# Stage ends, first products and the final scaling of a two-layer streaming encoder reordered, and the inverse row sums spread by ScalarE

## What is computed

```python
def sink_softmax(logits, sink):
    m = jnp.maximum(jnp.max(logits, axis=-1, keepdims=True), sink)
    p = jnp.exp(logits - m)
    return p / (jnp.sum(p, axis=-1, keepdims=True) + jnp.exp(sink - m))

def conv_ffn(x, left, g, w_gate, w_up, cw, cb, w_down):
    xn = rms_norm(x, g)
    a = xn @ w_gate
    ap = jnp.concatenate([left, a], axis=1)
    ac = cb + sum(ap[:, j:j + L] * cw[j] for j in range(CONV_W))
    return (jax.nn.gelu(ac) * (xn @ w_up)) @ w_down, ap[:, -(CONV_W - 1):]

# per layer: h = h + attention(rms_norm(h)) @ w_o ; h = h + conv_ffn(h)
# end: rms_norm(h, g_final)
```

## Time and profile before

| | us |
|---|---|
| median of 3 runs (2988.56 to 2990.41) | 2989.19 |
| profiled execution | 2989.44 |
| its span | 2987.7 |
| TensorE busy | 2881.6 |
| prompts, layers 0 and 1 | 208 and 319 |

### The profile page before, as it was taken

How to read it: one execution, slowest core, us unless ns; L and a number is a source line. 1 busy time by engine, 2 the same in 40 slices (tenths; PEclk the granted TensorE clock), 3 DMA queues, 4 the chain that set the end, 5 groups by cost and what they waited for, 6 DMA issues and landing times. The chain is left out here.

```text
span 2987.7 us, 47694 instructions
## 1 busy us (share of the span) xinstructions
PE 2881.6 (96%) x18405; PEld 2707.4 (91%) x18405; DVE 1521.5 (51%) x2719; ACT 676.0 (23%) x1324; POOL 902.0 (30%) x861
## 2 busy tenths in 40 slices
PE   7999999999999999999888999999999999999997
PEld 6987798999999999988588777789999999999996
DVE  5046615544444444445588777532644444444445
ACT  3035511000000000013466655532100000000002
POOL 4233333222222222224123754323222222222221
PEclk8999999999999999999999999999999999999998
DMA  4430011111111111114012000021111111111111
GB/s 122 65 96 10 21 29 36 37 37 40 42 42 42 42 42 42 42 35 129 1 35 72 10 11 9 20 79 36 36 43 42 42 36 41 42 42 42 35 35 73
DMA packets 178196, 129.66 MB, mean 43 GB/s; under 512 B 25313, under 2 KB 168353, under 8 KB 177846
## 3 DMA queue, kind: packets, MB, share of 16 engines
q1 hardware_dynamic: 178066, 127.90, 14.9%
HBM read 111.13 MB, written 15.16 MB: 42 GB/s over the span
## 5 line engine op out<-in xcount | busy, mean ns | idle before, releaser
L665 DVE TENSOR_TENSOR h<-h,ps_gemm 128x1170 f32<-128x1170 f32 x192 | 263.7, 1373 | 407.8 <-PE ps_gemm L1433 232.4
L1195 POOL CAST w_hi<-w_raw 128x1024 fp32r<-128x1024 f32 x120 | 125.1, 1042 | 1130.2 <-PE ps_gemm L1417 624.9
L1417 PE MATMUL ps_gemm<-xh,w_hi 128*128 128x390 f32 x1920 | 448.1, 341 | 0.0
L1417 PE MATMUL ps_gemm<-xh,w_lo 128*128 128x390 f32 x1920 | 448.1, 342 | 0.0
L1417 PE MATMUL ps_gemm<-xl,w_hi 128*128 128x390 f32 x1920 | 446.1, 340 | 0.0
L1417 PEld LDWEIGHTS ps_gemm<-xh,w_hi 128*128 128x128 f32 x1920 | 352.5, 189 | 0.0
L1417 PEld LDWEIGHTS ps_gemm<-xl,w_hi 128*128 128x128 f32 x1920 | 349.4, 189 | 0.0
L1417 PEld LDWEIGHTS ps_gemm<-xh,w_lo 128*128 128x128 f32 x1920 | 349.1, 189 | 0.0
L1198 POOL TENSOR_TENSOR w_lo<-w_raw,w_hi 128x1024 fp32r<-128x1024 f32 x120 | 288.1, 2401 | 17.4
L1381 PE MATMUL ps_gemm<-xl,w_hi 128*128 128x390 f32 (+1 forms) x1152 | 272.5, 345 | 0.0
L1433 PE MATMUL ps_gemm<-gu_lo,w_hi 128*128 128x390 f32 x1056 | 248.7, 344 | 0.0
(11 more groups left out here) (393 smaller groups left out, 4346.5 us busy)
## 6 DMA issues: line engine op xcount, KB each, us to landing
w_raw<-in_w_gate SPq DMA_DIRECT2D x44, 512.0 KB, 3.8
w_raw<-in_w_up SPq DMA_DIRECT2D x44, 512.0 KB, 3.8
w_raw<-in_w_down SPq DMA_DIRECT2D x44, 512.0 KB, 3.3
w_raw<-in_w_in_b SPq DMA_DIRECT2D x13, 512.0 KB, 4.1
w_raw<-in_w_qkv_a SPq DMA_DIRECT2D x10, 512.0 KB, 4.0
residual_park<-h SPq DMA_DIRECT2D x1, 4680.0 KB, 13.7
h<-residual_park SPq DMA_DIRECT2D x8, 585.0 KB, 8.2
out<-yt SPq DMA_DIRECT2D x9, 512.0 KB
```

Source lines behind the costliest of these rows:

```text
L665: dve.tensor_tensor(c3(h[:, m, :]), c3(h[:, m, :]), pse(j), ALU.add).then_inc(evac[j % 2], 1)
L1195: pool.tensor_copy(whi[c % 3][:], raw[c % 2][:]).then_inc(w_hi_done, 1)
L1417: mm = pe.matmul(ps[j % 2][:, m_, 0:CH], w[:, k, :], x[:, k, m_ * CH:(m_ + 1) * CH], start=(k == 0 and w is wh and x is XH), stop=(k == KT ...
```

## The change

- `gemm` with `gate`: for all eight channel tiles first the two products with XH (waiting for `xh_done`), then the product with XL (waiting for `xl_done`). In the norms ahead of the feed-forward networks the addition of the seventh square moves behind the third low half.
- Feed-forward: the GELU is multiplied by R before the up product is there; the product is then taken out of PSUM times that, in three pieces. The last loop iteration is written out; context transposes stand in it in three groups of two, taken by VectorE alone. `last_down` starts its first two output blocks with the first hidden tile of the pair before it waits for the second.
- Attention: ScalarE copies the inverse row sums to a 128x128 block (`repeat_inverse`), TensorE transposes that in place of the two matmuls; VectorE's reciprocal waits for an older copy.
- Index stage: `take_qi(2)` and `take_qi(3)` stand three score additions earlier.
- End: transposes and VectorE's multiplication by the gain start before the mean of squares is known; all first halves go first, ScalarE scales them later; second halves as before. The last square is not added but summed by a second matmul.

```diff
+            dve.memset(gb[:, T - 2:T], 0.0).then_inc(pad_ga, 1)
             def up(F, u, j, i):
-                wait_at(dve, gul_done, F, 2, i)
-                wait_at(dve, mm_done, j + 1, 12, i)
-                dve.tensor_tensor(c3(gb[:]), pse(j), c3(R[:]), ALU.mult).then_inc(evac[j % 2], 1)
-                wait_at(dve, evac[j % 2], j // 2 + 1, 6, i)
-                wait_at(dve, gel_done, F + 1, 2, i)
-                dve.tensor_tensor(gb[:, 0:MAIN], gb[:, 0:MAIN], ac[:, 0:MAIN], ALU.mult)
-                dve.tensor_tensor(gv, gv, acs, ALU.mult).then_inc(prod_done, 1)
+                wait_at(dve, gel_done, F + 1, 2, i)
+                dve.tensor_tensor(ac[:, 0:MAIN], ac[:, 0:MAIN], R[:, 0:MAIN], ALU.mult)
+                dve.tensor_tensor(acs, acs, Rs, ALU.mult).then_inc(ac_scaled, 1)
+                wait_at(dve, gul_done, F, 2, i)
+                wait_at(dve, ac_scaled, F + 1, 2, i)
+                wait_at(dve, mm_done, j + 1, 12, i)
+                dve.tensor_tensor(gb[:, 0:2 * CH]..., src[:, 0:2, 0:CH], ac[:, 0:2 * CH]..., ALU.mult)
+                dve.tensor_tensor(gb[:, 2 * CH:MAIN], src[:, 2, 0:MAIN - 2 * CH], ac[:, 2 * CH:MAIN], ALU.mult)
+                dve.tensor_tensor(gv, src[:, 2, ...], acs, ALU.mult).then_inc(evac[j % 2], 1)
...
             def pair(F, jb, i, ctx):
...
                 for m in range(3, KT):
                     residual(dve, jb + 1 + m, m, i)
+                ctx(0)
                 up(F, 0, jb + 9, i)
+                ctx(2)
                 gate(F + 1, 1, jb + 10, i)
                 up(F + 1, 1, jb + 11, i)
+                ctx(4)
...
             def gemm(c, j, x_hi, x_lo, n=P, gate=None, between=None):
+                if gate is not None:
+                    for k in range(KT):
+                        pe.wait_ge(xh_done, gate + k + 1)
+                        for w in (wh, wl):
+                            for m in range(NCH):
+                                pe.matmul(..., w[:, k, 0:n], x_hi[:, k, ...], ...)
+                    for k in range(KT):
+                        pe.wait_ge(xl_done, gate + k + 1)
+                        for m in range(NCH):
+                            mm = pe.matmul(..., wh[:, k, 0:n], x_lo[:, k, ...], ...)
...
-                ctx_transposes(m // 2, g_ctx)
-                down(c0 + 4 + 6 * it, jb + 12 * it, 0, gu0 + FT)
+                job(c, jl, 0, 0)
+                down(c + 1, jl + 1, 0, gu0 + FT - 2)
+                ctx_transposes(m // 2, g_ctx, 0)
+                job(c + 3, jl + 9, 0, 0)
+                ctx_transposes(m // 2, g_ctx, 2)
+                job(c + 4, jl + 10, 0, 0)
+                job(c + 5, jl + 11, 0, 0)
+                ctx_transposes(m // 2, g_ctx, 4)
+                last_down(c + 6, jl + 12, gu0 + FT)
+            def last_down(c, j, f_done):
...
+                pe.wait_ge(gul_done, f_done - 1)
+                for m_ in range(2):
+                    pe.wait_ge(evac[(j + m_) % 2], (j + m_) // 2)
+                    products(m_, 0)
+                pe.wait_ge(w_split, c + 2)
+                pe.wait_ge(gul_done, f_done)
+                for m_ in range(KT):
+                    if m_ >= 2:
+                        pe.wait_ge(evac[(j + m_) % 2], (j + m_) // 2)
+                        products(m_, 0)
+                    products(m_, 1).then_inc(mm_done, 1)
...
-                            pe.wait_ge(p_rinv, NU * layer + i + 1)
-                            for r in range(2):
-                                mm = pe.matmul(tb[j % 2][HD * r:HD * (r + 1), P * k:P * (k + 1)],
-                                               stat(2, i, r).to_broadcast([P, HD]), ident[:], start=True, stop=True)
+                            pe.wait_ge(p_wide, NU * layer + i + 1)
+                            mm = pe.transpose(tb[j % 2][:, P * k:P * (k + 1)],
+                                              inverse(layer, i).rearrange("p r d -> p (r d)"), ident[:])
...
+                def repeat_inverse(i):
+                    act.wait_ge(p_rinv, NU * layer + i + 1)
+                    if i >= 2:
+                        act.wait_ge(p_tr, transposed(layer, i - 2))
+                    copy(inverse(layer, i), stat(2, i).unsqueeze(2).to_broadcast([P, 2, HD])).then_inc(p_wide, 1)
...
                     part(parts[1])
+                    if 1 <= n <= NU:
+                        repeat_inverse(n - 1)
                     if n < NU:
                         probs(n, 1)
...
                         dve.wait_ge(p_exp, 2 * (NU * layer + n))
+                        if n >= 4:
+                            dve.wait_ge(p_wide, NU * layer + n - 3)
                         dve.reciprocal(stat(2, n - 1), stat(1, n - 1)).then_inc(p_rinv, 1)
...
-                for n in range(half // 2 * i, half // 2 * (i + 1)):
+                n0, n1 = half // 2 * i, half // 2 * (i + 1)
+                for n in range(n0, n1 - 3):
                     add_scores(n)
                 take_qi(2 + i)
+                for n in range(n1 - 3, n1):
+                    add_scores(n)
...
+            for gi in range(3):
+                turn_final(gi)
+            pe.wait_ge(acc_done, 7 * 4 + 6)
+            pe.wait_ge(sq_done, 8 * 5)
             for tt in range(9):
-                mm = pe.matmul(far[0][:, tt:tt + 1], x4["acc"][:, c], mean_w[:, 0:1], start=True, stop=True)
+                pe.matmul(far[0][:, tt:tt + 1], x4["acc"][:, c], mean_w[:, 0:1], start=True, stop=False)
+                mm = pe.matmul(far[0][:, tt:tt + 1], x4["sq0"][:, c], mean_w[:, 0:1], start=False, stop=True)
             mm.then_inc(mm_done, 1)
+            for gi in range(3, 18):
+                turn_final(gi)
...
+            for tt in range(9):
+                g = G_FIN + tt
+                act.wait_ge(tr_out[g % 2], g // 2 + 1)
+                y = x12["yt"][:, tt, 0:512]
+                copy(y, y, rs_f[:, tt:tt + 1]).then_inc(fin_scaled, 1)
...
             for gi in range(18):
-                tt, kk = divmod(gi, 2)
+                kk, tt = divmod(gi, 9)
+                if gi == 3:
+                    dve.wait_ge(rs_out, 1)
+                    dve.reciprocal(rs_f[:], rs_f[:]).then_inc(r_done, 1)
...
+                if kk == 0:
+                    dve.tensor_tensor(y, tb[g % 2][:], gain, ALU.mult).then_inc(tr_out[g % 2], 1)
+                else:
+                    dve.scalar_tensor_tensor(y, tb[g % 2][:], rs_f[:, tt:tt + 1], gain, ALU.mult, ALU.mult).then_inc(tr_out[g % 2], 1)
```

More of the change, by code:

```diff
@@ L516, in stat, with inverse @@
             return rreg["stats"][:, o:o + 2] if r is None else rreg["stats"][:, o + r:o + r + 1]
+        def inverse(layer, i):
+            return (hreg["ri_b"] if layer else x4["ri_a"])[:, i % 2, :, :]
         def near_at(i):
@@ L680, in ffn_act @@
             for u in range(2):
-                tile(F0 + u, u, None, j0)
-            with act.Fori(0, FT // 2 - 1) as i:
+                tile(F0 + u, u, None, j0 + 1 + 2 * u, j0)
+            with act.Fori(0, FT // 2 - 2) as i:
                 for u in range(2):
-                    tile(F0 + 2 + u, u, i, j0 + 4 + 9)
+                    tile(F0 + 2 + u, u, i, j0 + 4 + 9 + 2 * u, j0 + 4 + 9)
+            jb = j0 + 4 + 12 * (FT // 2 - 2)
+            for u in range(2):
+                tile(F0 + FT - 2 + u, u, None, jb + 9 + 2 * u, jb + 9)
         def ffn_dve(dve, l, j0):
@@ L1359, in _ @@
             split_ffn(C_FFB, 3)
-            add_squares(4)
+            for k in (1, 3, 5):
+                add_one(4, k)
         @block.tensor
@@ L1375, in gemm @@
                 wh, wl = whi[c % 3], wlo[c % 3]
+                if gate is not None:
[3 more added lines that the diff above has]
+                            for m in range(NCH):
+                                pe.matmul(ps[j % 2][0:n, m, 0:CH], w[:, k, 0:n], x_hi[:, k, m * CH:(m + 1) * CH],
+                                          start=(k == 0 and w is wh), stop=False)
+                    for k in range(KT):
+                        pe.wait_ge(xl_done, gate + k + 1)
+                        for m in range(NCH):
+                            mm = pe.matmul(ps[j % 2][0:n, m, 0:CH], wh[:, k, 0:n], x_lo[:, k, m * CH:(m + 1) * CH],
+                                           start=False, stop=(k == KT - 1))
+                    mm.then_inc(mm_done, 1)
+                    return
                 for k in range(KT):
-                    if gate is not None:
-                        pe.wait_ge(xl_done, gate + k + 1)
                     for w, x in ((wh, x_hi), (wh, x_lo), (wl, x_hi)):
@@ L2078, in _ @@
             act.activation(rs_f[:], far[0][:, 0:9], ACT.Sqrt, bias=eps[:, 0:1]).then_inc(rs_out, 1)
+            act.wait_ge(r_done, 13)
+            for tt in range(9):
+                g = G_FIN + tt
+                act.wait_ge(tr_out[g % 2], g // 2 + 1)
+                y = x12["yt"][:, tt, 0:512]
+                copy(y, y, rs_f[:, tt:tt + 1]).then_inc(fin_scaled, 1)
         @block.vector
```

104 lines of the change are left out of this document (59 added, 45 removed).

## The result

The changed kernel takes 2974.72 us as a median of four runs (2969.67 to 2975.06), the kernel before 2989.8 of four (2988.56 to 2991.28); the ratio is 0.9945, with a 95% interval of 0.9928 to 0.9963. It is faster by half a per cent, not by the 1.5% of the forecast (2943), and the time lies above the forecast's range. The profiled execution took 2974.74 us, 14.70 less than the profiled one of before (2989.44), with a span of 2973.0. From here on, times of stages come from these two traces.

What follows compares the result with a forecast made beforehand. The prediction took TensorE as the bound, busy 2881.6 of 2987.7 us, the prompts by its issue. Terms -23.4 - 3.4 - 14.4 - 7 + 2 = -46.2 took 2989.4 to 2943 us, range 2932 to 2960.

Steps and rivals of the forecast that it cites:

- Part 1: Inverse row sums in the prompts: a sixth transpose replaces two matmuls, saving 0.16 us per unit, -23.4 us (-14 to -24).
- the cover: Prompts: TensorE needs ScalarE's copy about 2.4 us later; without this cover each unit loses 0.16 us plus up to 0.3.
- The first: Prompts: TensorE waits for ScalarE's copies or evacuations; half or less of Part 1 left, 2955 to 2964 us; chance 0.11.
- The slower one: Prompts lose the full clock as transposes replace 584 matmul records; half the prompts at 1.2 GHz gives 3068 us; chance 0.04.
- signs of being wrong: TensorE waiting for ScalarE's wide copy, a granted clock below 1 in the prompts, or DMA above 408 GB/s throughout the stores.
- Parts 2 and 3: First product of a stage: -3.4 us (0 to -5.4); ends of the feed-forward networks: -14.4 us (-11 to -17).
- Part 4: Index queries: gaps before the third and fourth tile shrink by 2.4 and 3.3 us; taken -7 us (-2.4 to -9).
- Part 5: Final scaling at the kernel's end: +2.9 us with means at the low clock, -1.1 at the full one; taken +2 us.
- the case that was taken: Final scaling: the means run at the low clock after a gap, +2.9 us worked out, +2 us taken.

## Why the prediction was wrong, point by point

**Part 1, size of the term.** The step counted the distance to the start of the next product and held that "the change to the narrower product is paid once, as now". TensorE after, one unit of the later part of the prompt:

```profile
314.25 0.77 PE L1546 MATMUL ps_tr<-ident,xa 128*128 128x128 f32 x5
314.85 0.27 PE L1542 MATMUL ps_tr<-ident,ri_a 128*128 128x128 f32 x1
315.05 0.66 PE L1572 MATMUL ps_near<-pta_v,vtok 128*64 128x128 f32 x8
315.64 0.49 PE L1565 MATMUL ps_near<-pta_x,vbd 128*128 128x128 f32 x2
```

Transposes to product is 315.05 - 314.25 = 0.80, just as worked out from the earlier trace rows. But the change has a second half: the first pair of products behind it takes 0.15 us from start to start, the later ones 0.10. Before, the inverse matmuls paid that; now the value products do: their eight records last 315.64 - 315.05 = 0.59 us instead of 0.54 in the earlier trace rows (from 305.59 to 306.13, where the next products begin). So a unit saves 0.11, not 0.16. The last unit's reciprocal against that of the thirteenth gives the same in layer 0: 60 units take 161.1 us instead of 167.4. Of 23.4 us, 15.5 were there by this; the runs gave 15.0.

**Part 1, the cover.** "TensorE needs the copy a whole unit later, about 2.4 us", and the wait "holds back nothing that could run". This is the step that failed: the overlap of ScalarE's copy with TensorE's work. The 2.4 us hold later in the prompt of layer 0, where the earlier trace rows lie: from the seventeenth unit on, the trace before has a median of 2.4 us between the end of a reciprocal and the moment when TensorE is free for that inverse. In the third to ninth units of both prompts it has 0.3 to 0.9 us (the fifth of layer 0 apart, whose reciprocal stands behind the mask settings). And the step asked what stands behind the copy in ScalarE's order, not what stands ahead of it: the first exponential of the next unit. In layer 0 that one waits for GpSimd's sink columns, and these for the output split, so the copies of the fourth to ninth unit start 1.6 to 1.7 us after their reciprocals begin; in layer 1, without that wait, 0.8 to 1.1.

From the fifth unit to the thirteenth VectorE's reciprocals stand 2.3 us apart before (193.92 to 212.25) and 3.9 after (193.97 to 225.24): 13 us lost in eight units, 1.2 of them in waits for the copy and most of the others at half clock. Layer 1 loses 3.5 us from its third to its eleventh unit, at the full clock. The half clock of layer 0 stood in no term of the sum.

**The rivals.** The first had the right cause, TensorE waiting for ScalarE's copy, with 11 in 100 and too small a price: at most 21 of part 1's 23.4 us lost (2964), where the prompts lost all of them and 5 us more. The slower one had the right kind of price, the clock in the prompts, but put it down to transposes, and so held the 0.98 of the earlier trace rows against it. Here the half clock followed waits for a late copy. I had priced each of them by itself; in the run the one brought on the other. Two of the signs of being wrong that the prediction named are in the trace after: TensorE waits for the wide copy (2.9 us in each prompt), and the clock in the prompt of layer 0 is 0.92.

The Trainium skill (TensorE: Matmul & The Clock Gate, Part 4: PE-mode transpose) has it that the full clock does not engage for transposes. The traces do not agree. At the end of the changed kernel TensorE does nothing but transposes from 2952.73 to 2965.16, and within them the clock rises to its full level and stays there (columns as in the earlier trace rows):

```profile
2953.00:2958.00 5.00, 5.00 (x23) 4.06 (x22) 3.25 (x6) 4.59 (x8) 0.00 (x0) 0.50 0.00 0
2958.20:2965.20 7.00, 6.11 (x38) 3.79 (x36) 6.70 (x11) 1.42 (x2) 0.00 (x0) 1.00 0.65 265
```

The prompts with the copy first and the settings spread, where transposes lie among other matmuls, were granted 0.99.

**Parts 2 and 3** held. TensorE after, first gate product of layer 0, and the end of that network:

```profile
502.69 2.64 PE L1410 MATMUL ps_gemm<-xl,w_hi 128*128 128x390 f32 x12
508.29 5.06 PE L1410 MATMUL ps_gemm<-xl,w_hi 128*128 128x390 f32 x11 [2.96 <-DVE xl L2176]
...
1330.41 0.82 PE L1521 MATMUL ps_tr<-ident,conv_ctx 128*18 128x128 f32 x6
1330.98 0.78 PE L1499 MATMUL ps_gemm<-gu_hi,w_hi 128*128 128x390 f32 x3
...
1334.98 0.78 PE L1499 MATMUL ps_gemm<-gu_hi,w_hi 128*128 128x390 f32 x3 [0.56 <-DVE gu_lo L762]
```

The wait moved to the low halves, as said, and a spell at half clock follows it (eleven matmuls take 5.06 us where twelve took 2.64). The wait inside the down products is 0.56 us where 0.7 was worked out; the 6.16 of the earlier trace rows, among the context transposes, is gone.

**Part 4** named the returning work and gave it no price. TensorE, ScalarE and VectorE after:

```profile
1454.11 1.77 PE L1764 MATMUL ps_far<-kit,qi 64*128 64x384 f32 x8 [1.71 <-issue]
1457.57 0.81 PE L1764 MATMUL ps_far<-kit,qi 64*128 64x320 f32 x4 [1.69 <-ACT rl L2099]
1460.26 2.74 PE L1764 MATMUL ps_far<-kit,qi 64*128 64x320 f32 x8 [1.88 <-ACT rl L2099]
...
1458.22 0.60 ACT L2099 ACTIVATE rl<-ps_far 128x512 f32<-128x512 f32 x1 [0.70 <-DVE scm L2372]
...
1453.92 10.17 DVE L2372 SCALAR_TENSOR_TENSOR scm<-rl,kitok,scm 128x896 f32<-128x896 f32 x9
```

The fourth query's gap is 1.71 instead of the 4.92 of the earlier trace rows (1.6 forecast), and the third's is gone. But nine additions now run back to back behind the query, ScalarE's buffers wait for them, and TensorE stands another 1.69 and 1.88 us for ScalarE. These waits are more than what 4.8 lacks to 7.

**Part 5** came out at +3.7, above the +2 that was taken and the +2.9 worked out for the half clock. The stretch of the means, and that of the stores:

```profile
2944.50:2958.00 13.50, 13.50 (x63) 12.56 (x63) 4.32 (x8) 5.09 (x9) 0.00 (x0) 0.50 0.00 0
...
2961.00:2972.00 11.00, 3.62 (x24) 2.20 (x21) 4.76 (x7) 0.00 (x0) 0.00 (x0) 0.83 1.03 420
```

The means ran at half clock, the case that was taken, and the end came 32.0 us after the last down product (31.2 worked out); in traces whose half clock ended sooner it came after 27.3 to 28.5 (27.2 worked out for the full clock). The stores moved 420 GB/s over 11 us, more than the 408 worked out from the earlier trace rows.

The Trainium skill (DMA: Bandwidth & Descriptors, Where 436 GB/s comes from) puts what the memory side of one core allows at about 358 GB/s; by its section Measured a core alone reached 425 on a read of 16 MB. The 420 here lie above the first and near the second.

## What to carry to other kernels

When a wait is moved to another engine, read that engine's order and name everything that now stands between the producer and the consumer, and what each of those waits for; then check the cover in the first and shortest units, not in one from the middle. Where a matmul's operand shape changes, take distances over the whole run up to the next change of shape, since a cost taken away on one side can turn up on the other. Where a bound TensorE will wait in several units in a row, price a stretch at half clock beside the waits: in layer 0 it came and cost more than they did, in layer 1 it did not come.

## What the hardware showed that I had not expected

- Waits of 0.25, 0.25 and 1.17 us in three neighbouring units were followed by 31 us at 1.2 GHz (two more waits, 0.80 and 0.40, lie inside them) in which TensorE was busy for 29.4 of 30.7 us; it came back to 2.4 GHz while doing the same kind of work. In the kernel before, one wait of 1.1 us in the same place was followed by none, and in layer 1 of the changed kernel eight waits of 0.25 to 0.47 us by none. What brings the stretch on and what sets its length was not settled: 20 to 34 us in the traces here.
- VectorE's reciprocal costs 157 ns for 2 columns and 946 for 128; ScalarE's copy of 128 columns takes 296 ns.
- In the prompts a product with a stationary operand of 64 columns starts 0.20 us after a transpose with one of 128 (314.85 to 315.05); these products run in pairs, and the next pair starts 0.15 us later, the following ones 0.10. Transposes in a row start 0.11 us apart.
